# Queries of two mixers projected with channels on the partitions instead of tokens, in a two-layer decoder trunk

## The chip, the cores and the metric

The kernel runs on one core of a Trainium2 chip. The time is the device time of one execution in microseconds. A core has five engines that run side by side and wait for each other by semaphores: TensorE (PE, matmuls), VectorE (DVE), ScalarE (ACT), GpSimd (POOL) and SyncE (SP, which starts transfers). Each engine takes its own instructions strictly in the order in which the program lists them. PE reads two operands, a stationary one (at most 128 by 128) that it loads first, and a moving one of at most 512 columns, and writes into one of eight banks (PSUM), each 128 by 512 float32. Every other engine works on 128 partitions at a time.

## The reference

Two layers. Each layer is

```
h = rmsnorm(x); proj = h @ w_in                      # 512 tokens x 1024 -> 3072 columns
a_u, a_v, b_q, b_k, b_v, b_g, c_q, c_k, c_v = split(proj)
y_a = gmlp(a_u, a_v)                                 # 4 heads of 64
y_b = silu(b_g) * head_norm(retention(rope(b_q), rope(b_k), b_v))     # 6 heads of 64
y_c = sliding_window_attention_with_sinks(rope16(c_q), rope16(c_k), c_v)  # 6 query heads, 2 key heads
x += rmsnorm([y_a | y_b | y_c] @ w_out)
x += rmsnorm((silu(h2 @ w_gate_ffn) * (h2 @ w_up)) @ w_down)           # h2 = rmsnorm(x)
x += sigmoid(x @ w_gate) * rmsnorm(p @ w_ple)
```

The attention mixer (called swa below) works in chunks of 128 queries against the chunk's own and the previous 128 keys; softmax includes a sink. Retention (ret) works in chunks of 128 as well, with a running state. `rope` turns pairs of channels of a head by an angle that grows with the token: all 64 channels of a head in retention, the first 16 in attention. Everything is float32; the large matmuls are made of three products of a high and a low part (`mm3`), with operands of the type float32r.

## The kernel before, in words

Tokens are in four tiles of 128. The matrix `w_in` is taken in groups of columns (`GROUPS`): keys and values of attention (`ckv`, 256 columns), its queries (`cq`, 384), then keys, queries and values of retention (`bk`, `bq`, `bv`, 384 each), the gMLP (`a`, 512) and the retention gate (`bg`, 384). A group of 384 or 512 columns is two strips of four 128-row blocks. A strip is loaded by SP into `raw` (two pieces), split by ACT into `w_hi` (L1411) and by DVE into `w_lo` (L1891, L1893), and then PE runs four blocks on it, one for each tile of tokens (`mm_in`): the stationary operand is a tile of h, the moving one the weights, and the result has tokens on the partitions. A block of a 384-column strip is 4 x 3 = 12 matmuls. There are three slots of split weights, so the split of a strip starts when the strip three before it is used up.

The small work of the mixers is laid between these blocks. `plan_mixers` is a table by units: unit u is the u-th block of a layer's projection, counted from 4 (the first block after `ckv`), and behind the block of unit u every engine finds the steps that the table puts there, in the order of the `put` calls. The table says nothing of times; each engine simply takes its own part of each step in that order and waits by semaphore for what it needs. The steps of chunk c of attention are: `swa_T` (PE transposes queries and keys of a tile, L1255 and L1257, ACT copies them to `cT`), `swa_cur` (scores against the own keys, L1273; ACT copies them to `prob`, L1674), `swa_prev` (scores against the previous keys into the same banks, L1273; DVE merges and takes the maximum, L2258 to L2263; ACT takes the exponentials, L1682), `swa_norm` (DVE, L2268 to L2270), `swa_PT` (PE transposes the probabilities, L1281; ACT copies them to `ptu`, L1688 and L1691), `swa_mask` (DVE multiplies the transposed ones by a triangle, `ptl`, L2279), `swa_o` (PE, L1294), and `swa_yhi`, `swa_ylo` (ACT L1382 and DVE L1941 split the result). In `swa_PT` ACT copies one half, waits for DVE's mask of the other half (`pt_masked0`) and copies that; the copy of `swa_cur` of the next chunk is behind it in ACT's order, and PE's `swa_prev` of that next chunk waits for this copy (`swa_S`).

Retention has `ret_T` (transposes of key and query, L1309), `ret_sc` (scores L1317; DVE multiplies by a triangle into `scm`, L2289), `ret_o` (L1329, L1333, L1338; DVE adds to the state, L2303, and sums squares, L2306), `ret_norm` and `ret_yT`. Keys and queries of retention are rotated by DVE straight out of the banks (`rope_full`, L1920 to L1924, four instructions for a tile). Queries of attention come by ACT to `cq` (L1738) and are rotated by DVE there (L1934 to L1937). gMLP has `gmlp_v` (DVE, L2321 to L2328, five instructions for a tile; POOL L1838 and L1839 take the root of the variance) and `gmlp_n` (POOL, L1847 to L1849).

In the second layer the first blocks stand between the last ones of the layer before: transposes of x (L1214), splits to `h_hi` (ACT L1449) and `h_lo` (DVE L1957), and the split of the first weight strips.

## Time and profile before

| | us |
|---|---|
| median of 3 runs | 1225.45 (1225.24 to 1225.57) |
| the profiled execution | 1225.42 |
| its span, first to last instruction | 1223.7 |
| PE busy | 1217.0 |
| DVE busy | 841.5 |
| ACT busy | 616.0 |
| POOL busy | 136.6 |
| mean granted TensorE clock | 1.00 |

The span is what the trace covers; the 1.7 us between it and the time lie before the first and behind the last instruction. The projection and mixers of the first layer lie between 10 and 178 us, those of the second between 616 and 785 us. A timeline's row has start, duration, engine, line, operation, output and inputs, shape and count, and behind it in brackets the idle time before it with what ended it. Durations of matmuls are modelled to their end and overlap; the distance between two starts is what one costs PE.

### The profile page before, as it was taken

Reading aid. Unit: us, or ns where it says so; the run is one execution under the profiler, and the core shown is the slowest. Engines: PE = TensorE matmul, PEld = TensorE weight load, DVE = VectorE, ACT = ScalarE, POOL = GpSimd, SP = SyncE. Lnnn points to the kernel's source line nnn. Section 1 sums busy time; section 2 is a strip of 40 time slices with the busy share of each in tenths; the row PEclk is TensorE's granted clock in tenths of the full one; section 3 lists DMA queues with packets and bytes.
Section 4 is the critical chain, followed back from the end, with each engine's and each line's share of the span. In section 5 each row is a group of like instructions: output and inputs, shape, how many; then the busy total and the mean of one; then the engine's idle time right before and its main releaser. Section 6 shows DMA issues by size and latency. Waiting matters only on the chain.

```text
span 1223.7 us, 20397 instructions
## 1 busy us (share of the span) xinstructions
PE 1217.0 (99%) x7873; PEld 1109.8 (91%) x7873; DVE 841.5 (69%) x1365; ACT 616.0 (50%) x1204; POOL 136.6 (11%) x208
## 2 busy tenths in 40 slices
PE   9999999999999999999999999999999999999998
PEld 8988888999999988888899889889999999888887
DVE  5685646888888853267976756468988887433788
ACT  7454435555555532237664544364655555422474
POOL 2003621100000000003030037020000000000120
PEclk9999999999999999999999999999999999999999
DMA  7322232233333354320242222231333333444001
GB/s 247 111 65 91 70 103 69 70 104 104 104 105 106 109 183 154 124 67 18 86 119 73 91 75 90 74 103 53 104 105 106 108 101 119 163 147 172 18 18 70
DMA packets 124464, 122.31 MB, mean 100 GB/s; under 512 B 5200, under 2 KB 108752, under 8 KB 124368
## 3 DMA queue, kind: packets, MB, share of 16 engines
q1 hardware_dynamic: 123680, 120.48, 31.4%
q8 instruction: 63, 1.03, 0.4%
q10 hardware_dynamic: 688, 0.53, 0.2%
q14 instruction: 33, 0.27, 0.1%
HBM read 118.90 MB, written 2.10 MB: 99 GB/s over the span
## 4 chain that ended last, share of the span: by engine, by line
PE 98%; DVE 1%; ACT 0%; POOL 0%; issue 0%; DVEq 0%; ACTq 0%
PE bank L1004 31%; PE bank L1006 30%; PE bank L1005 30%; PE bank L1214 2%; PE bank L1273 1%; PE bank L1294 1%; PE bank L1333 1%; PE bank L1317 1%; PE bank L1309 0%; PE bank L1281 0%; PE bank L1329 0%; PE bank L1338 0%; PE bank L1224 0%; PE bank L1359 0%; PE bank L1255 0%; DVE ple_n L2196 0%
## 5 line engine op out<-in xcount | busy, mean ns | idle before, releaser
L1004 PE MATMUL bank<-w_hi,h_hi 128*128 128x384 f32 (+2 forms) x564 | 200.4, 355 | 0.8 <-DVE w_lo L1893 0.7
L1005 PE MATMUL bank<-w_lo,h_hi 128*128 128x384 f32 (+2 forms) x564 | 194.6, 345 | 0.0
L1891 DVE TENSOR_TENSOR w_lo<-raw,w_hi 128x1024 fp32r<-128x1024 f32 x70 | 83.6, 1233 | 133.7 <-ACT w_hi L1411 133.5
L1004 PE MATMUL bank<-h_hi,w_hi 128*128 128x256 f32 x568 | 161.0, 284 | 0.1
L1006 PE MATMUL bank<-h_hi,w_lo 128*128 128x256 f32 x568 | 160.7, 283 | 0.0
L1005 PE MATMUL bank<-h_lo,w_hi 128*128 128x256 f32 x568 | 160.7, 283 | 0.0
L1006 PE MATMUL bank<-w_hi,h_lo 128*128 128x384 f32 (+2 forms) x468 | 157.5, 336 | 0.0
L1411 ACT ACTIVATE w_hi<-raw 128x1024 fp32r<-128x1024 f32 x70 | 70.6, 1053 | 160.7 <-PE bank L1006 160.6
L1006 PE MATMUL bank<-w_hi,mid_lo 128*128 128x512 f32 x352 | 137.0, 389 | 0.0
L1004 PE MATMUL bank<-T_hi,w_hi 128*128 128x256 f32 x448 | 126.8, 283 | 0.0
L1005 PE MATMUL bank<-T_lo,w_hi 128*128 128x256 f32 x448 | 126.8, 283 | 0.0
L1006 PE MATMUL bank<-T_hi,w_lo 128*128 128x256 f32 x448 | 126.8, 283 | 0.0
L1004 PEld LDWEIGHTS bank<-w_hi,h_hi 128*128 128x128 f32 x564 | 106.2, 188 | 15.1 <-issue 5.2
L1005 PEld LDWEIGHTS bank<-w_lo,h_hi 128*128 128x128 f32 x564 | 106.3, 189 | 6.2
L1004 PEld LDWEIGHTS bank<-h_hi,w_hi 128*128 128x128 f32 x568 | 109.0, 192 | 0.6 <-issue 0.5
L1005 PEld LDWEIGHTS bank<-h_lo,w_hi 128*128 128x128 f32 x568 | 109.0, 192 | 0.1
L1006 PEld LDWEIGHTS bank<-h_hi,w_lo 128*128 128x128 f32 x568 | 109.0, 192 | 0.0
L1790 POOL TENSOR_SCALAR tiny<-tiny 128x1 f32<-128x1 f32 x24 | 20.0, 835 | 755.5 <-ACT junk_f L1614 683.0
L1505 ACT ACTIVATE w_hi<-w_sum 128x512 fp32r<-128x512 f32 x112 | 70.4, 629 | 52.5 <-DVE w_sum L2034 51.2
L1006 PEld LDWEIGHTS bank<-w_hi,h_lo 128*128 128x128 f32 x468 | 88.1, 188 | 3.1
L1004 PEld LDWEIGHTS bank<-T_hi,w_hi 128*128 128x128 f32 x448 | 86.0, 192 | 0.0
L1005 PEld LDWEIGHTS bank<-T_lo,w_hi 128*128 128x128 f32 x448 | 86.0, 192 | 0.0
(294 smaller groups left out, 2909.3 us busy)
## 6 DMA issues: line engine op xcount, KB each, us to landing
raw<-in_w_ffn_in SPq DMA_DIRECT2D x88, 512.0 KB, 3.9
raw<-in_w_ffn_out SPq DMA_DIRECT2D x44, 512.0 KB, 4.2
raw<-in_w_in SPq DMA_DIRECT2D x40, 384.0 KB, 3.8
raw<-in_w_out SPq DMA_DIRECT2D x16, 512.0 KB, 3.8
gw<-in_w_gate SPq DMA_DIRECT2D x16, 512.0 KB, 3.4
raw<-in_w_in SPq DMA_DIRECT2D x10, 512.0 KB, 4.6
raw<-in_w_ple SPq DMA_DIRECT2D x4, 512.0 KB, 5.9
x<-in_x_in SPq DMA_DIRECT2D x3, 512.0 KB, 6.9
```

Of the source, the lines that this page charges most:

```text
L1004: pe.matmul(out_ap, a_hi, b_hi, start=start, stop=False, skip_group_check=True)
L1005: pe.matmul(out_ap, a_hi, b_lo, start=False, stop=False, skip_group_check=True)
L1006: return pe.matmul(out_ap, a_lo, b_hi, start=False, stop=stop, skip_group_check=True)
L1214: last = pe.transpose(t_bank(layer, stage, m, half)[:, k * P:(k + 1) * P], src[:, kk * P:(kk + 1) * P], T_("ident"))
L1273: last = pe.matmul(swa_bank(c, g)[:, j * P:(j + 1) * P], cT[rows(g), j, ts(c)], cT[rows(g), 3, ts(k0)], start=True, stop=True, skip_group_ ...
L1294: last = pe.matmul(swa_bank(c, 1)[rows(g), 0:BW], values[:, g, :], probs[:, 3 * g:3 * g + 3, :], start=(i == 0), stop=(i == len(pairs) - 1 ...
L1317: last = pe.matmul(banks[4 + g][:, j * P:(j + 1) * P], kqT[rows(g), 0, j, :], kqT[rows(g), 1, j, :], start=True, stop=True, skip_group_che ...
L1333: last = pe.matmul(banks[4][:, cols], scm[:, g, j, :], bv[:, c, cols], start=(c == 0), stop=True, skip_group_check=True)
L1411: last = act.activation(w_hi[slot_of(g)][:, j * n + cols.start:j * n + cols.stop], raw[q % RAWS][:, cols], ACT.Copy, scale=1.0 if col is N ...
L1505: act.activation(hi, whole, ACT.Copy).then_inc(st_hi, 1)
L1790: pool.tensor_scalar(e_post[n % 2], ss_post[n % 2][:, 0:1], EPS, None, ALU.add).then_inc(post_e, 1)
L1891: last = dve.tensor_tensor(lo, raw[q % RAWS][:, cols], hi, ALU.subtract)
```

## The change

Queries of both mixers are now projected turned: the weights are the stationary operand (128 columns of them), h of all 512 tokens is the moving one, and the result has channels on the partitions. For this the queries' columns are put together (`turned_last`, on the host) and taken as three strips of 256 columns (`qa`, `qb`, `qc`), each two blocks of 128 channels; blocks 0 to 2 are attention, 3 to 5 retention. A unit is now half a block (4 x 3 = 12 matmuls of 512 columns). ACT copies a block to `q_raw`, POOL's queue starts four transfers that write it to `q_turn` with the halves of each rotated range exchanged, and DVE makes x cos + exchanged x sin from tables (`turns`) that SP loads. The copies, rotations and transposes of queries before are gone, and the tokens' norm factor enters at the exponentials (`s_q`, `s_qn`). In the second layer the first block is made for three tiles of tokens (`q_most`) ahead of the last block of `ckv`, and for the last tile behind it. A layer's projection has 48 units in place of 52; the table of steps is moved to match. The variances of `gmlp_v` go to two buffers in turn. The masks of chunks 0 and 1 are put one unit earlier.

```diff
-    "cq": (2 * AW + 4 * BW, BW),
+    "qa": (2 * AW + 3 * BW, 2 * P),
+    "qb": (2 * AW + 3 * BW + 2 * P, 2 * P),
+    "qc": (2 * AW + 3 * BW + 4 * P, 2 * P),
...
-    "bq": (2 * AW, BW),
...
+    for i in range(2 * len(TURNED)):
+        put((6, 8, 10, 12, 16, 17)[i], "q_rope", i)
+    put(8, "swa_T")
     for c in range(TILES):
-        put(10 + c, "swa_T", c)
         u = (13, 18, 23, 28)[c]
         put(u, "swa_cur", c)
...
         put(u + (2, 1, 2, 2)[c], "swa_norm", c)
+        put(u + (5, 4, 4, 5)[c], "swa_mask", c)
         put(u + 5, "swa_PT", c)
-        put(u + (5, 5, 3, 5)[c], "swa_mask", c)
         put(u + 7, "swa_o", c)
...
-        u = (33, 37, 41, 45)[c]
+        u = (31, 35, 39, 43)[c]
         for step, name in zip((0, 2, 3), ("ret_T", "ret_sc", "ret_o")):
             put(u + step, name, c)
-        put(41 + c, "gmlp_v", c)
-        put(42 + c, "gmlp_n", c)
+        put(37 + c, "gmlp_v", c)
+        put(38 + c, "gmlp_n", c)
...
+            add("q_most", lay=nxt)
+            mm(ins[0], 3, nxt)
             mm(ins[1], 0, nxt)
             mm(ins[1], 1, nxt)
-            mm(ins[0], 3, nxt)
...
+            def mm_turned(layer, i, half, cols):
+                g = layer * NS + SIDX[("in", TURNED[i // 2], 0)]
+                if half == 0 and i < 4:
+                    pe.wait_ge(*evac(layer, "ckv", i))
+                elif half == 0:
+                    pe.wait_ge(q_evac, 6 * layer + i - 3)
...
+                for k in range(4 * half, 4 * half + 4):
+                    last = mm3(banks[i % 4][:, cols], hi[:, k, c], lo[:, k, c], h_hi[:, k, cols], h_lo[:, k, cols],
+                               k == 0, k == KD - 1)
...
+                    if name == "bk":
+                        pe.wait_ge(q_evac, 6 * layer + (5, 6, 3, 4)[m])
...
+                        act.wait_ge(mm_done, mm_count(layer, strip, m))
+                        if n > 2:
+                            act.wait_ge(q_roped, n - 2)
+                        act.activation(q_raw[b][:], banks[i % 4][:, :], ACT.Copy).then_inc(q_evac, 1)
...
+                    pool.wait_ge(q_evac, 6 * layer + i + 1)
+                    for r in (0, HD):
+                        for d in (r, r + half):
+                            src = 2 * r + half - d
+                            pool.dma_start(q_turn[b][d:d + half, :],
+                                           q_raw[b][src:src + half, :]).then_inc(q_turned[b], 16)
...
+                    dve.tensor_tensor(dst, q_raw[b][:], cos_q[which][:], ALU.mult)
+                    dve.wait_ge(q_turned[b], 64 * (3 * layer + i // 2 + 1))
+                    step(dve.tensor_tensor(q_turn[b][:], q_turn[b][:], sin_q[which][:], ALU.mult))
+                    done(dve.tensor_tensor(dst, dst, q_turn[b][:], ALU.add), q_roped)
...
-                    for i, src in enumerate((bk, bq)):
-                        for j in range(3):
-                            last = pe.transpose(banks[4 + i][:, j * P:(j + 1) * P],
-                                                src[:, c, j * P:(j + 1) * P], T_("ident"))
+                    for j in range(3):
+                        last = pe.transpose(banks[4][:, j * P:(j + 1) * P], bk[:, c, j * P:(j + 1) * P], T_("ident"))
...
-                    if m or layer:
-                        dve.wait_ge(gm_r, layer * TILES + m)
-                    done(dve.tensor_reduce(gvar, heads(vsq[:], A_HEADS), AX.X, ALU.add), gm_v)
+                    if m > 1 or layer:
+                        dve.wait_ge(gm_r, layer * TILES + m - 1)
+                    done(dve.tensor_reduce(gvar[m % 2], heads(vsq[:], A_HEADS), AX.X, ALU.add), gm_v)
```

The first place at which instructions move, on DVE in each layer, is around the mask of chunk 1 (`ptl_103`). In DVE's order before, the last instruction of the norm (`prob_101`), one split of weights (`w_lo_79`) and then the mask:

```order
L2270 TENSOR_TENSOR prob_101<-prob_101,tiny 128x768 [waits dve_step]
L1893 SCALAR_TENSOR_TENSOR w_lo_79<-raw_74,mix_col,w_hi_76 128x384 [waits hi_ready]
L1893 SCALAR_TENSOR_TENSOR w_lo_79<-raw_74,mix_col,w_hi_76 128x384
L1893 SCALAR_TENSOR_TENSOR w_lo_79<-raw_70,mix_col,w_hi_76 128x384 [waits hi_ready]
L1893 SCALAR_TENSOR_TENSOR w_lo_79<-raw_70,mix_col,w_hi_76 128x384
L2279 TENSOR_TENSOR ptl_103<-bank,tab 128x384 [waits swa_PT]
L2279 TENSOR_TENSOR ptl_103<-bank,tab 128x384 [waits pt_copied1]
L1893 SCALAR_TENSOR_TENSOR w_lo_80<-raw_71,mix_col,w_hi_77 128x384 [waits hi_ready]
L1893 SCALAR_TENSOR_TENSOR w_lo_80<-raw_71,mix_col,w_hi_77 128x384
```

In DVE's order of the change the norm and the same split stand there too (line numbers are 69 to 81 higher), then four instructions for tile 0 of retention's keys as those of the first four rows here, and then, for tiles 1 and 2 (`rope_a`, `rope_b` and `bk`; L1988 and L1989 were L1920 and L1921), up to the mask and the start of tile 3:

```order
L1988 TENSOR_TENSOR rope_a<-bank,tab 128x384 [waits b_roped,mm_done]
L1989 TENSOR_TENSOR rope_b<-bank,tab 128x384
L1991 TENSOR_TENSOR bk<-rope_a,rope_b 128x6x32 [waits evac_dve]
L1992 TENSOR_TENSOR bk<-rope_a,rope_b 128x6x32
L1988 TENSOR_TENSOR rope_a<-bank,tab 128x384 [waits b_roped,mm_done]
L1989 TENSOR_TENSOR rope_b<-bank,tab 128x384
L1991 TENSOR_TENSOR bk<-rope_a,rope_b 128x6x32 [waits evac_dve]
L1992 TENSOR_TENSOR bk<-rope_a,rope_b 128x6x32
L2360 TENSOR_TENSOR ptl_103<-bank,tab 128x384 [waits swa_PT]
L2360 TENSOR_TENSOR ptl_103<-bank,tab 128x384 [waits pt_copied1]
L1988 TENSOR_TENSOR rope_a<-bank,tab 128x384 [waits b_roped,mm_done]
L1989 TENSOR_TENSOR rope_b<-bank,tab 128x384
```

The key rotations of tiles 0 to 2, which stood in the units of chunk 0 before, now stand between chunk 1's norm and chunk 1's mask; that of tile 3 is behind the mask.

The second place, on DVE as well, is the triangle product of retention's chunk 2 (`scm`). Before, it stands behind the gMLP step of tile 1 (`uv` to `vn` to `vsq`), ahead of that of tile 2:

```order
L2321 TENSOR_REDUCE tiny<-uv 128x4 [waits evac_act]
L2322 TENSOR_SCALAR tiny<-tiny 128x4 [waits dve_step]
L2323 TENSOR_TENSOR vn<-uv,tiny 128x256 [waits dve_step]
L2325 TENSOR_TENSOR vsq<-vn 128x256 [waits dve_step]
L2328 TENSOR_REDUCE tiny<-vsq 128x4 [waits gm_r,dve_step]
L2289 TENSOR_TENSOR scm<-bank,tab 128x384 [waits ret_sc]
L2289 TENSOR_TENSOR scm<-bank,tab 128x384
L2321 TENSOR_REDUCE tiny<-uv 128x4 [waits evac_act]
```

In the change it stands behind the steps of tiles 1, 2 and 3 and a split of weights of `w_out` (`w_lo_78`); the first row here is the end of tile 2's step:

```order
L2409 TENSOR_REDUCE tiny<-vsq 128x4 [waits gm_r,dve_step]
L1960 TENSOR_TENSOR w_lo_78<-raw_74,w_hi_75 128x1024 [waits hi_ready]
L1960 TENSOR_TENSOR w_lo_78<-raw_70,w_hi_75 128x1024 [waits hi_ready]
L2402 TENSOR_REDUCE tiny<-uv 128x4 [waits evac_act]
L2403 TENSOR_SCALAR tiny<-tiny 128x4 [waits dve_step]
L2404 TENSOR_TENSOR vn<-uv,tiny 128x256 [waits dve_step]
L2406 TENSOR_TENSOR vsq<-vn 128x256 [waits dve_step]
L2409 TENSOR_REDUCE tiny<-vsq 128x4 [waits gm_r,dve_step]
L2370 TENSOR_TENSOR scm<-bank,tab 128x384 [waits ret_sc]
L2370 TENSOR_TENSOR scm<-bank,tab 128x384
```

Two steps of gMLP and one split of weights have moved from behind the triangle product of chunk 2 to ahead of it.

## Rows read from the trace of the kernel before

**Rows 1.** Page: busy time of an engine, share of the span, instructions
```profile
PE 1217.0 (99%) x7873; PEld 1109.8 (91%) x7873; DVE 841.5 (69%) x1365; ACT 616.0 (50%) x1204; POOL 136.6 (11%) x208
```
**Rows 2.** Page: the chain that ended last, shares of the span by engine
```profile
PE 98%; DVE 1%; ACT 0%; POOL 0%; issue 0%; DVEq 0%; ACTq 0%
```
**Rows 3.** Timeline of PE: 384-column matmuls, then 512-column ones of w_out
```profile
22.88 0.34 PE L1004 MATMUL bank<-w_hi,h_hi 128*128 128x384 f32 x1
...
37.27 0.34 PE L1006 MATMUL bank<-w_hi,h_lo 128*128 128x384 f32 x1
...
180.56 0.39 PE L1004 MATMUL bank<-w_hi,y_hi 128*128 128x512 f32 x1
...
185.78 0.39 PE L1006 MATMUL bank<-w_hi,y_lo 128*128 128x512 f32 x1
```
**Rows 4.** Chain in order of time, first layer: start, duration, engine, line
```profile
37.61 0.33 PE bank L1255 x3
40.14 0.33 PE bank L1255 x3
...
111.83 1.28 PE bank L1333 x12
...
116.62 0.66 PE bank L1309 x6
```
**Rows 5.** Timeline of DVE at the start of layer two
```profile
603.68 3.25 DVE L1893 SCALAR_TENSOR_TENSOR w_lo<-raw,mix_col,w_hi 128x256 fp32r<-128x256 f32 x8
...
619.98 2.20 DVE L1893 SCALAR_TENSOR_TENSOR w_lo<-raw,mix_col,w_hi 128x384 fp32r<-128x384 f32 x4
...
622.61 1.28 DVE L1957 TENSOR_TENSOR h_lo<-bank,h_hi 128x512 fp32r<-128x512 f32 x2
```
**Rows 6.** Timeline of PE there, behind the last transposes
```profile
623.35 0.39 PE L1004 MATMUL bank<-w_hi,h_hi 128*128 128x256 f32 x1
```
**Rows 7.** Chain in order of time: swa_o of chunk 0, swa_prev of chunk 2
```profile
64.08 0.80 PE bank L1294 x4
...
75.16 0.87 PE bank L1273 x12
```
**Rows 8.** Timeline of DVE: key rotations to mask 0, norm 1 to split
```profile
55.59 0.55 DVE L1920 TENSOR_TENSOR rope_a<-bank,tab 128x384 f32<-128x384 f32 x1
...
60.75 1.01 DVE L2279 TENSOR_TENSOR ptl<-bank,tab 128x384 f32<-128x384 f32 x2
...
63.27 1.05 DVE L2258 COPY_PREDICATED prob<-later_m,bank 128x384 f32<-128x384 int32 x2
...
68.28 0.17 DVE L2268 TENSOR_TENSOR tiny<-tiny 128x6 f32<-128x6 f32 x1 [2.12 <-ACT tiny L1684]
...
69.59 2.20 DVE L1893 SCALAR_TENSOR_TENSOR w_lo<-raw,mix_col,w_hi 128x384 fp32r<-128x384 f32 x4
```
**Rows 9.** Timeline of ACT: copies of ptu and prob, chunk 2 to 3
```profile
87.50 0.49 ACT L1691 ACTIVATE ptu<-bank 128x384 f32<-128x384 f32 x1
87.89 0.87 ACT L1674 ACTIVATE prob<-bank 128x384 f32<-128x384 f32 x2
```
**Rows 10.** Timeline of DVE: retention's chunk 1, gMLP tiles 0 and 2
```profile
129.28 0.72 DVE L2303 TENSOR_TENSOR state<-state,bank 64x192 f32<-64x192 f32 x2 [2.48 <-PE bank L1338]
...
130.50 0.41 DVE L2321 TENSOR_REDUCE tiny<-uv 128x4 f32<-128x256 f32 x1
...
132.12 0.42 DVE L2328 TENSOR_REDUCE tiny<-vsq 128x4 f32<-128x256 f32 x1
...
139.97 0.41 DVE L2321 TENSOR_REDUCE tiny<-uv 128x4 f32<-128x256 f32 x1
...
142.70 2.35 DVE L1891 TENSOR_TENSOR w_lo<-raw,w_hi 128x1024 fp32r<-128x1024 f32 x2
```
**Rows 11.** Transfers issued: KB each, median us from issue to landing
```profile
raw<-in_w_in SPq DMA_DIRECT2D x40, 384.0 KB, 3.8
...
later_m<-in_later SPq DMA_DIRECT2D x1, 64.0 KB, 9.3
```
**Rows 12.** Timeline of SP's queue: one issue near the start
```profile
4.38 0.43 SPq L976 DMA_DIRECT2D tab<-in_table  x1
```

More of the change, by code:

```diff
@@ L200, in plan_schedule @@
         mm(o[0], 0)
-        for u in (52, 53):
-            if u == 53:
+        for u in (48, 49):
+            if u == 49:
                 mm(o[1], 0)
@@ L519, in build_trunk @@
     r_mix = [small(1) for _ in range(TILES)]
+    s_q = [small(1) for _ in range(TILES)]
+    s_qn = [small(1) for _ in range(TILES)]
     nsnk = small(C_HEADS)
@@ L533, in build_trunk @@
     gmu = small(4)
-    gvar = small(4)
+    gvar = [small(4) for _ in range(2)]
     gvt = small(4)
@@ L579, in build_trunk @@
     ck_roped = sem("ck_roped")
-    cq_roped = sem("cq_roped")
+    turns_loaded = [sem(f"turns_loaded{i}") for i in range(2)]
+    q_evac = sem("q_evac")
+    q_turned = [sem(f"q_turned{i}") for i in range(2)]
+    q_roped = sem("q_roped")
+    q_scaled = sem("q_scaled")
+    q_zeroed = sem("q_zeroed")
     b_roped = sem("b_roped")
@@ L1161, in block_of @@
                     pe.wait_ge(lo_ready, 2 * (g + 1))
-                if kind == "in":
+                if kind == "in" and strip[1] in TURNED:
+                    block = 2 * TURNED.index(strip[1]) + m // 2
+                    last = mm_turned(layer, block, m % 2, slice(S - P if layer and block == 0 else 0, S))
+                elif kind == "in":
                     last = mm_in(layer, g, strip, m)
@@ L1246, in _ @@
                     gate_product(layer, e[1], e[2:] or (0, 1))
+                elif kind == "q_most":
+                    for half in range(2):
+                        mm_turned(layer, 0, half, slice(0, S - P))
                 elif kind == "swa_T":
-                    c = e[1]
-                    pe.wait_ge(ck_roped, layer * TILES + c + 1)
-                    pe.wait_ge(cq_roped, layer * TILES + c + 1)
-                    if c > 1:
-                        pe.wait_ge(swa_cT, layer * TILES + c - 1)
-                    for j in range(3):
-                        pe.transpose(banks[6 + c % 2][:, j * P:(j + 1) * P], cq[c % 2][:, j * P:(j + 1) * P],
-                                     T_("ident"))
-                    pe.transpose(banks[6 + c % 2][:, 3 * P:4 * P], ck[:, c, :],
-                                 T_("ident")).then_inc(swa_T, 1)
+                    pe.wait_ge(ck_roped, (layer + 1) * TILES)
+                    for c in range(TILES):
+                        last = pe.transpose(banks[6][:, c * P:(c + 1) * P], ck[:, c, :], T_("ident"))
+                    last.then_inc(swa_T, 1)
                 elif kind in ("swa_cur", "swa_prev"):
@@ L1313, in _ @@
                     c = e[1]
-                    pe.wait_ge(ret_kqT, layer * TILES + c + 1)
+                    pe.wait_ge(ret_kT, layer * TILES + c + 1)
+                    if c == 0:
+                        pe.wait_ge(q_roped, 6 * layer + 6)
                     for j in range(3):
                         for g in range(2):
-                            last = pe.matmul(banks[4 + g][:, j * P:(j + 1) * P], kqT[rows(g), 0, j, :],
-                                             kqT[rows(g), 1, j, :], start=True, stop=True,
+                            last = pe.matmul(banks[4 + g][:, j * P:(j + 1) * P], kT[rows(g), j, :],
+                                             qT[rows(g), j, ts(c)], start=True, stop=True,
                                              skip_group_check=True)
@@ L1699, in _ @@
                     act.wait_ge(ret_T, layer * TILES + c + 1)
-                    for i in range(2):
-                        last = act.activation(kqT[:, i, :, :],
-                                              banks[4 + i][:, 0:BW].rearrange("p (k t) -> p k t", k=3),
-                                              ACT.Copy)
-                    last.then_inc(ret_kqT, 1)
+                    act.activation(kT[:], banks[4][:, 0:BW].rearrange("p (k t) -> p k t", k=3),
+                                   ACT.Copy).then_inc(ret_kT, 1)
                 elif kind == "ret_o":
@@ L1909, in pre, with rope_full @@
                                                   op0=ALU.mult, op1=ALU.mult), xn_ready)
-            def rope_full(layer, which, m):
-                dst = (bk, bq)[which]
+            def rope_full(m):
                 xr = banks[m][:, 0:BW].rearrange("p (h s d) -> p h s d", h=6, s=2)
@@ L2363, in _, with turned_last @@
                         dve.wait_ge(mm_done, mm_count(layer, strip, m))
-                        rope_full(layer, DVE_EVAC.index(name), m)
+                        rope_full(m)
+def turned_last(w):
+    a, bq, bk, bv, bg, cq, ckv = np.split(w, np.cumsum([2 * AW] + 5 * [BW]), 2)
+    cq = cq.reshape(*w.shape[:2], C_KV, C_HEADS // C_KV, HD).transpose(0, 1, 3, 2, 4).reshape(cq.shape)
+    return np.concatenate([a, bk, bv, bg, cq, bq, ckv], 2)
 def heads_in_pairs(w):
@@ L2385 @@
     depth = w_in.shape[0]
-    table, later = small_tables()
+    table, later, turns = small_tables()
     values = {
```

136 lines of the change are left out of this document (90 added, 46 removed).

## The prediction

> **What bounds the kernel.** I read the busy shares first: PE works 1217.0 of the 1223.7 us of the span, DVE 841.5 [rows 1]. Then the chain that ended last: 98% of it is PE and DVE holds 1% [rows 2]. So the time is PE's work plus the few places where it waits, and each term below is either work taken from PE or a wait given to it. The profiled execution took 1225.42 us, 1.7 more than its span and 0.03 less than the median of the runs, so the sum is made against 1225.42. The granted clock is 1.00 throughout, which is the 2.4 GHz level; the work ahead of the changed stages stays as dense, so I leave it there.
>
> **PE's work, projection.** Two matmuls of 384 columns 83 apart start at 22.88 and 37.27: 0.1734 us each. Two of 512 columns 23 apart start at 180.56 and 185.78: 0.2270 each [rows 3]. The queries were 2 groups x 8 blocks x 12 = 192 matmuls of 384 columns, 33.29 us; they become 6 x 2 x 12 = 144 of 512, 32.68 us. Layer 1: -0.6. In layer 2 the first block is cut in two: 24 matmuls for three tiles (384 columns, 4.16 us) and 24 for the last tile (128 columns), beside 120 of 512 (27.24 us). The trace has no float32r matmul of 128 columns. By the slope of columns between 384 and 512 one would cost 0.067; if it were as dear as one of 384 it would cost 0.173. The nearest row is the smaller matmul of retention, 12 in 1.28 us, 0.107 each although it has 64 columns [rows 4]; I take that: 2.57 us (ends 1.6 and 4.2). Layer 2 is 33.97 us, +0.7.
>
> The row of 64 columns shows that a matmul doesn't fall with its columns below some cost. The Trainium skill, "TensorE: Matmul & The Clock Gate", section on LDWEIGHTS, gives P/1.2 ns for loading P columns of stationary operand, 107 ns for 128, and with it this row agrees; its section on the back-to-back issue gap says about 81 ns for N=128, by which the last tile would cost 1.9 us in place of 2.57 and the sum would be 0.6 lower.
>
> **PE's work, transposes.** Each layer had four groups (`swa_T`) of four transposes; one group stays, for the keys. From one group to the next 2.53 us pass [rows 4], of which 12 x 0.1734 = 2.08 are a block: 0.45 a group, so -1.35 a layer. Retention's six transposes for a chunk take 0.66 us [rows 4]; three stay, -0.33 for each of four chunks, -1.32 a layer. PE's work together: layer 1 -3.28, layer 2 -1.99, in all -5.3 us.
>
> **Start of layer 2.** DVE splits the first strip of queries there. A split of a 384-column piece is four instructions in 2.20 us, of 256-column strips eight in 3.25 [rows 5]; the strip of the change is of the second kind, so DVE comes 1.05 later to `h_lo` of tile 2. That instruction starts at 622.61 and its first half is done at 623.25; PE wants it at 623.35 [rows 5, 6]. Spare is 0.1, so PE stands 0.9 to 1.05: +1.0, once.
>
> **Mask of chunk 1, both layers.** Three key rotations now stand ahead of it on DVE. I count from the end of `swa_o` of chunk 0, 64.08 + 0.80 = 64.88, since the order on PE between it and `swa_prev` of chunk 2 keeps its length; PE starts that one at 75.16, 10.28 later [rows 7]. DVE's chain from 64.88: to the norm's start at 68.28, 3.4 (0.3 less if ACT's exponentials come straight behind its copy of y, since rotations no longer hold DVE's maximum); norm to the split 1.31; split 2.1 to 2.2; three rotations, 60.75 - 55.59 = 5.16; half of a mask 0.5 [rows 8]. Then ACT's second copy to `ptu` (0.39 to the next start) and its copy of the scores, 0.87 [rows 9]; this last is what PE waits for. Sum 13.4 to 13.8 against 10.28: PE stands 3.1 to 3.5 us, and as some of it may be off the path I take 3.2; +6.4 for two layers. Queued behind the mask on DVE are the last key rotation and the maximum for chunk 2; both have time while PE stands. The end from below is 0 for each, if DVE runs further ahead of PE than I count.
>
> **`scm` of retention's chunk 2, both layers.** Two gMLP steps and a split for `w_out` are now ahead of it. From the end of `ret_o` 1, DVE: state and sum 1.22; three gMLP steps at 2.0 each (130.50 to 132.12 + 0.42) or, as at 139.97 to 142.70, 2.73; a split of 2.35; `scm` 1.0, the same operation and size as a mask [rows 8, 10]. That is 10.5 to 12. PE meanwhile: a block of 512 columns 2.72, three transposes 0.33, two blocks of 2.08, scores 0.87, a block 2.08: 10.2. Stall 0 to 1.8, I take 1.2: +2.4 for two layers. The second variance buffer takes from DVE's last instruction of a gMLP step the wait for POOL's root, for which reason I count the steps without such waits; beyond that it is worth nothing by itself, since nothing of PE's hangs on gMLP there.
>
> **Transfers of POOL's queue.** The trace has no transfer from POOL's queue. From above and below: in SP's queue an issue takes 0.43 [rows 12], landings take 3.8 at the median for 384 KB and 9.3 at the start for 64 KB, which is the size here [rows 11]. Four issues and the common landing are 5.5 us; with the long one 11. What waits is DVE's rotation of block 3; behind it in DVE's order stand the merge and maximum of chunk 0, behind these ACT's exponentials, and behind them in ACT's order the copy of the last query block, whose bank PE needs for the second block of keys. PE takes from the end of block 3 to there four half blocks (10.9), a block of keys (2.08) and two scores (0.87 each) [rows 3, 7]: 14.7. The others need a copy (0.49 for 384 columns [rows 9], 0.65 for 512), two DVE instructions of 512 columns (0.55 each for 384, 1.5 together), merge to exponentials 68.28 - 63.27 = 5.0 [rows 8], and a copy, 0.65: 7.8, with some 0.6 as an estimate for the hand-overs 8.4. That leaves 6.3 us for the transfers before PE stands. I take 5.5: hidden, 0. If they take longer, each microsecond costs PE one in each layer. The first layer's extra strips, ACT's copies of queries (it is busy 50% of the span) and the loads of tables (four of 256 KB a layer) lie beside PE's work: 0.
>
> The Trainium skill, "DMA: Bandwidth & Descriptors", section on the anatomy of a GpSimd-path DMA, gives about 2.0 us + bytes/436e3 each, thus by estimate 8.6 us for four of 64 KB one behind another, 2.3 past the slack; no row here shows it. "SBUF — State Buffer" adds that some DVE modes starve the writing of descriptors, which no run shows either.
>
> **Sum.** -5.3 + 1.0 + 6.4 + 2.4 + 0 = +4.5; 1225.42 + 4.5 = 1229.9 us. About 0.2%, 2.45 us, is what a measurement of this kernel tells from no change.
>
> **Rivals.**
> A. The masks and `scm` are in time: the new waits don't come, or only the 1.0 and a rest. For it: DVE is busy 69% of the span, and before the norm of chunk 1 it idled 2.12 us waiting for ACT [rows 8], a wait that may shrink by more than my 0.3. The point is the mask of chunk 1: from a chain of 10.28 us down the 6.4 are gone, and they are the price. Against: the wait of 2.12 ends with ACT, whose work stays, and 5.16 us of rotations are more than it. Time 1225.4 - 5.3 + 0 to 2.4 = 1220.1 to 1222.5. Chance 0.20. This is the case in which the change gains.
> B. Half of the stalls, which is what the lower ends of my counts leave, if PE's way is longer by hand-overs of its own: 1225.4 - 5.3 + 1 + 3.2 + 1.2 = 1225.5, 1223 to 1227.9: no difference. Chance 0.16.
> C. Late transfers: the place is the bank of the last query block, the point is a landing over 6.3 us after the copy, the price (d - 6.3) x 2. At d = 8.6 as with slow landings, +4.6: 1234.5; at 11, +9: 1239. Against: SP's landings of 3.8. Chance 0.14, slower still than mine.
> D. The forecast: 1227.9 to 1233, chance 0.50.
>
> Slower by over 0.2%: C and D, 0.64; within: 0.16; faster: 0.20. The range reaches from inside A to C, 1221.5 to 1235; the likeliest case's own is 1227.9 to 1233.
>
> **What the changed profile would show.** PE busy falls by some 5 us to about 1212, its idle time rises from 6.7 to about 16. In the chain, PE's `swa_prev` of chunk 2 follows ACT's copy to `prob`, behind DVE's mask, in both layers, with 3 us of wait each; without these waits the term of 6.4 is wrong. The score product of retention's chunk 2 is followed by DVE's gMLP steps and split, and `ret_o` 2 waits about 1 us. At the start of layer 2 `h_lo` of tile 2 holds the third `ckv` block for 1 us. The 24 matmuls of 128 columns start 0.107 apart. Each fourth transfer of a query block has landed under 6.3 us after ACT's copy, and PE never waits for `q_evac` at the keys; a longer landing there means case C. A span that falls while all DVE steps come late would prove the order on PE to have more slack than 10.28.

## The result and the profile after

The changed kernel takes 1235.65 us (median of four runs, 1234.17 to 1236.11), the one before 1225.45: ratio 1.0081, 95% interval 1.0064 to 1.0099. It is slower, as forecast, but by 10.2 us in place of 4.5, and outside the range of 1221.5 to 1235.0. The page of the profile after, busy time and share of the span of each engine:

```profile
span 1233.6 us, 20244 instructions
PE 1217.7 (99%) x7753; PEld 1098.2 (89%) x7753; DVE 849.5 (69%) x1353; ACT 617.4 (50%) x1210; POOL 168.9 (14%) x276
```

The share of PE is 99% as in [rows 1], and says nothing of what happened. The chain that ended last does: PE had 98% of it [rows 2].

```profile
PE 93%; DVE 4%; ACT 1%; issue 1%; POOL 0%; DVEq 0%; ACTq 0%
```

The view of waits, for PE: who waited, for whom, the sum in us, how often, the longest. These five of its rows matter; the second and the fifth were there before with 1.2 and 0.7, and the rows left out differ from before by 0.3 us or less.

```profile
PE bank L1324 <- ACT prob L1722: 7.3, 2, 3.6
PE bank L1277 <- DVE still L2014: 1.2, 1, 1.2
PE bank L1380 <- DVE scm L2370: 1.1, 2, 0.6
PE bank L1036 <- DVE h_lo L2025: 0.8, 1, 0.8
PE bank L1036 <- DVE ple_n L2264: 0.7, 2, 0.4
```

All three waits that the prediction named are there, and no other new one: 7.3 + 1.1 + 0.8 = 9.2 us. PE's idle time, span less busy, went from 6.7 to 15.9 us, which is the same 9.2. The rest of the result is PE's busy time: it should have fallen by 5.3 and rose by 0.7. The windows of the same trace show why (start and end of a stretch, its length, busy time of PE, PEld, DVE, ACT, POOL, then the granted clock):

```profile
85.00:91.00 6.00, 5.50 (x24) 5.06 (x24) 5.45 (x11) 2.88 (x6) 0.00 (x0) 0.50 0.24 67
92.00:97.00 5.00, 5.00 (x30) 4.35 (x27) 1.09 (x4) 3.45 (x14) 0.00 (x0) 1.00 0.14 50
699.00:703.00 4.00, 4.00 (x20) 3.71 (x18) 3.52 (x7) 1.89 (x4) 0.00 (x0) 0.57 0.16 26
```

Behind each of the two waits at the scores of chunk 2 (they end at 85.50 and 698.50) the clock stands at 0.50, the 1.2 GHz level: for 6.8 us in layer 1 (84.7 to 91.5), the first 0.8 of them still idle, and for 3.4 us in layer 2 (699.1 to 702.5). The rows of PE there:

```profile
85.50 1.65 PE L1324 MATMUL bank<-cT 64*128 64x128 f32 x12 [3.63 <-ACT prob L1722]
87.08 0.69 PE L1036 MATMUL bank<-w_hi,h_hi 128*128 128x384 f32 x1
87.56 0.52 PE L1037 MATMUL bank<-w_lo,h_hi 128*128 128x384 f32 x1
87.88 0.52 PE L1038 MATMUL bank<-w_hi,h_lo 128*128 128x384 f32 x1
```

The twelve score matmuls take 1.65 us, 0.87 before [rows 7], and 384-column matmuls start 0.32 apart and not 0.1734 [rows 3]. PE works for 6.0 and 3.4 us of these at half speed, which costs 3.0 and 1.7, together 4.7 us. Idle time and slow clock are 13.9 us, and the span grew by 9.9 (1233.6 - 1223.7). So 4.0 us of work were saved net; this last number is what is left over and not a measurement of its own. `best6` below measures the saving without new waits. Another 0.4 us is outside the span (2.2 between span and time, 1.7 before).

The wait at the mask, followed on DVE:

```profile
75.03 0.17 DVE L2349 TENSOR_TENSOR tiny<-tiny 128x6 f32<-128x6 f32 x1 [2.40 <-ACT tiny L1733]
...
76.33 2.20 DVE L1962 SCALAR_TENSOR_TENSOR w_lo<-raw,mix_col,w_hi 128x384 fp32r<-128x384 f32 x4
78.44 0.55 DVE L1988 TENSOR_TENSOR rope_a<-bank,tab 128x384 f32<-128x384 f32 x1
...
80.22 0.56 DVE L1988 TENSOR_TENSOR rope_a<-bank,tab 128x384 f32<-128x384 f32 x1
...
82.01 0.56 DVE L1988 TENSOR_TENSOR rope_a<-bank,tab 128x384 f32<-128x384 f32 x1
...
83.61 1.01 DVE L2360 TENSOR_TENSOR ptl<-bank,tab 128x384 f32<-128x384 f32 x2
```

Against [rows 8]: norm, split, three rotations 1.78 us apart (from the first to the mask 83.61 - 78.44 = 5.17, forecast 5.16), mask. ACT waits for it and copies:

```profile
84.19 0.49 ACT L1740 ACTIVATE ptu<-bank 128x384 f32<-128x384 f32 x1 [5.05 <-DVE ptl L2360]
84.58 0.87 ACT L1722 ACTIVATE prob<-bank 128x384 f32<-128x384 f32 x2
```

From the end of `swa_o` 0 (71.5) to the end of this copy (85.45) are 13.95 us; PE wanted it after 10.4 (85.50 - 3.63 - 71.5).

The rows that answer to the remaining terms: `scm` of retention's chunk 2, and PE behind it; `h_lo` of tile 2 in layer 2; the first of 24 matmuls of 128 columns and the 512-column one behind the last.

```profile
144.08 2.54 DVE L1960 TENSOR_TENSOR w_lo<-raw,w_hi 128x1024 fp32r<-128x1024 f32 x2
...
148.95 1.02 DVE L2370 TENSOR_TENSOR scm<-bank,tab 128x384 f32<-128x384 f32 x2
```
```profile
150.03 0.49 PE L1380 MATMUL bank<-state,qT 128*128 128x128 f32 x2 [0.56 <-DVE scm L2370]
...
628.76 0.39 PE L1036 MATMUL bank<-w_hi,h_hi 128*128 128x256 f32 x1 [0.83 <-DVE h_lo L2025]
...
638.77 0.22 PE L1036 MATMUL bank<-h_hi,w_hi 128*128 128x128 f32 x1
...
641.40 0.44 PE L1036 MATMUL bank<-h_hi,w_hi 128*128 128x512 f32 x1
```

The 24 take 2.63 us, 0.110 each (0.107 was taken from a 64-column row of [rows 4]). And the transfers of POOL's queue, which no row of before showed: four issues a block, and from the page's list of transfers size and landing.

```profile
40.95 2.05 POOL L1870 DMA_DIRECT2D q_turn<-q_raw  x4 [3.88 <-ACT q_raw L1781]
```
```profile
q_turn<-q_raw POOLq DMA_DIRECT2D x24, 64.0 KB, 2.0
q_turn<-q_raw POOLq DMA_DIRECT2D x24, 16.0 KB, 2.0
```

An issue takes 0.5 us, a landing 2.0 at the median and 3.5 at most; DVE's product waits until 44.26, 3.6 us after the copy's end at 40.66. DVE waits three times for such a landing, 6.2 us together, PE never.

### The profile page after: what moved, and what is told of

It is laid out like the page before. It is cut to its first block, busy times and chain, and to the rows that moved or that the text cites. A ratio compares the mean times of both kernels' runs of the same rounds, so it can differ in the third digit from the quotient of the medians.

```text
span 1233.6 us, 20244 instructions
## 1 busy us (share of the span) xinstructions
PE 1217.7 (99%) x7753; PEld 1098.2 (89%) x7753; DVE 849.5 (69%) x1353; ACT 617.4 (50%) x1210; POOL 168.9 (14%) x276
## 4 chain that ended last, share of the span: by engine, by line
PE 93%; DVE 4%; ACT 1%; issue 1%; POOL 0%; DVEq 0%; ACTq 0%
PE bank L1036 29%; PE bank L1038 29%; PE bank L1037 29%; PE bank L1267 2%; PE bank L1324 1%; PE bank L1345 1%; PE bank L1384 1%; DVE w_lo L1962 1%; ACT prob L1731 0%; PE bank L1368 0%; PE bank L1380 0%; DVE w_lo L1960 0%; PE bank L1389 0%; PE bank L1332 0%; PE bank L1277 0%
## 5 line engine op out<-in xcount | busy, mean ns | idle before, releaser
L1036 PE MATMUL bank<-h_hi,w_hi 128*128 128x256 f32 (+2 forms) x672 | 200.6, 299 | 0.1
L1038 PE MATMUL bank<-h_hi,w_lo 128*128 128x256 f32 (+2 forms) x672 | 200.0, 298 | 0.0
L1037 PE MATMUL bank<-h_lo,w_hi 128*128 128x256 f32 (+2 forms) x672 | 199.9, 297 | 0.0
L1036 PE MATMUL bank<-w_hi,h_hi 128*128 128x384 f32 (+2 forms) x436 | 158.4, 363 | 1.4 <-DVE h_lo L2025 0.8
L1037 PE MATMUL bank<-w_lo,h_hi 128*128 128x384 f32 (+2 forms) x436 | 153.1, 351 | 0.0
L1036 PEld LDWEIGHTS bank<-h_hi,w_hi 128*128 128x128 f32 x672 | 128.6, 191 | 4.1 <-issue 0.5
L1038 PE MATMUL bank<-w_hi,h_lo 128*128 128x384 f32 (+2 forms) x340 | 115.9, 341 | 0.0
L1036 PEld LDWEIGHTS bank<-w_hi,h_hi 128*128 128x128 f32 x436 | 83.1, 191 | 16.3 <-issue 6.1
L1037 PEld LDWEIGHTS bank<-w_lo,h_hi 128*128 128x128 f32 x436 | 83.2, 191 | 6.3
L1038 PEld LDWEIGHTS bank<-T_hi,w_lo 128*128 128x128 f32 x448 | 86.0, 192 | 0.0
```

What stands on the lines that cost most here:

```text
L1036: pe.matmul(out_ap, a_hi, b_hi, start=start, stop=False, skip_group_check=True)
L1037: pe.matmul(out_ap, a_hi, b_lo, start=False, stop=False, skip_group_check=True)
L1038: return pe.matmul(out_ap, a_lo, b_hi, start=False, stop=stop, skip_group_check=True)
```

## The experiments

Two theories stood at the start. By the first, called A in most expectations, the loss is DVE's order (one mask behind three rotations), and the slow clock follows from the idle. By the second, other parts of the change (turned blocks, transfers, a second buffer) have a share. Sixteen kernels were run. Where nothing else is said an experiment is an edit of the changed kernel's table of steps.

**Where the mask stands.** Three kernels move the mask of chunk 1 alone (`mold` has also the mask of chunk 2 one unit earlier).

```diff
-        put(u + (5, 4, 4, 5)[c], "swa_mask", c)
+        put(u + (5, 5, 3, 5)[c], "swa_mask", c)     # mold: behind 4 rotations
+        put(u + (5, 3, 4, 5)[c], "swa_mask", c)     # m21:  behind 2
+        put(u + (5, 2, 4, 5)[c], "swa_mask", c)     # m20:  behind 1
```

> The change with its masks at the old units (one later for chunks 1, one earlier for 2): the mask of chunk 1 is now behind all four key rotations. Theory A (each rotation ahead of the mask costs PE its 1.78 us): the wait at the scores of chunk 2 grows from 3.6 to 5.4 us in each layer, 3.6 us more in all, 1239 us; the mask of chunk 2 ahead of its transposes' neighbours costs nothing. Rival B: the last key rotation was in the wait's shadow anyway; same as the change, 1235.5.

> Mask of chunk 1 one unit earlier on DVE: behind the key rotations of tiles 0 and 1 (1.78 us less ahead of it than in the change). Theory A: PE waits 3.6 - 1.8 = 1.8 us at the scores of chunk 2 in each layer, so 3.6 us less than the change; if an idle of 1.8 us is too little to bring the clock down, another 5 are saved: 1227; if it isn't, half the slow stretch stays: 1229.5. Rival B (the clock has nothing to do with the wait): 1232.0 with the same two slow stretches of 6.4 and 3.3 us.

> Mask of chunk 1 two units earlier on DVE: behind the key rotation of tile 0 instead of those of tiles 0 to 2 (2 x 1.78 us less ahead of it). Theory A (the loss is the mask: 7.3 us of waiting at the previous-key scores of chunk 2, and the stretch at the 1.2 GHz level behind it comes from that idle): the wait falls below 0.5 us per layer, the granted clock stays 1.00, time 1235.65 - 7.3 - 5 = about 1223.5 us. Rival B (the clock falls for another reason, such as the denser 512-column stretch ahead of it): the waits go but the clock still falls, about 1228.4. Rival C (the rotations that now stand behind the mask hold the banks that the value blocks need): waits of 1 to 2 us at the blocks of bv in each layer, 1225.5 to 1227.5.

Measured: `mold` 1239.68 us (ratio 1.0116, 1.0101 to 1.0131), `m21` 1230.78 (1.0045, 1.0030 to 1.0060), `m20` 1233.15 (1.0064, 1.0048 to 1.0079). The wait at the scores of chunk 2 was 5.43 us a layer behind four rotations, 3.63 behind three, 1.85 behind two: 1.78 to 1.80 for each rotation, as theory A has it. With one it is gone, but `m20` is slower than `m21` and far from the 1223.5 expected, which neither of its rivals foresaw. Its largest wait of PE, and DVE's split and norm of chunk 2 with PE behind them:

```profile
PE bank L1332 <- DVE prob L2351: 5.7, 2, 2.8
```
```profile
85.83 2.74 DVE L1962 SCALAR_TENSOR_TENSOR w_lo<-raw,mix_col,w_hi 128x512 fp32r<-128x512 f32 x4
...
94.56 0.96 DVE L2351 TENSOR_TENSOR prob<-prob,tiny 128x768 f32<-128x768 f32 x1
...
95.58 0.88 PE L1332 MATMUL bank<-tab,prob 128*128 128x128 f32 x6 [2.83 <-DVE prob L2351]
```

PE now stands at the transposes of chunk 2 (L1332) until DVE has done that chunk's norm. In DVE's order between the two norms are two splits (2.2 and 2.7 us), four rotations, a mask and the maximum, and behind the maximum DVE waits for ACT's exponentials (3.1 us). That is more than PE's work takes from the one norm to the other; in the change the wait at the scores had hidden this. The mask was the first of two late links of one overfull stretch.

**The two smaller waits.** `m20gm` puts the gMLP steps two units later, and `best1` has, on top, the low part of h of tile 2 ahead of the split of the first strip of queries in layer 2.

```diff
-        put(37 + c, "gmlp_v", c)
-        put(38 + c, "gmlp_n", c)
+        put(39 + c, "gmlp_v", c)
+        put(40 + c, "gmlp_n", c)
...
-            add("conv", SIDX[ins[1]], lay=nxt)
             mm(ins[0], 0, nxt)
             add("T", "mix", 2, lay=nxt)
             add("pre", "mix", 2, lay=nxt)
+            add("conv", SIDX[ins[1]], lay=nxt)
```

> As the one with the mask behind one rotation, and the gMLP steps two units later, so that the triangle product of retention's chunk 2 stands ahead of the steps of tiles 2 and 3 and of the split for w_out. Theory A: the two waits of 0.6 and 0.5 us go, 1.1 less than that kernel, 1222.4. Rival: the gMLP's last steps come later and hold the gMLP product or the norms of retention in the w_out stretch; no gain or up to 2 us lost, 1223.5 to 1225.5.

> As the one before, and in layer 2 the low part of h of tile 2 stands ahead of the split of the first strip of queries on ACT and DVE. Theory A: the third ckv block of layer 2 no longer waits, 1.0 us less, 1221.4. Rival: the split of 3.25 us is now too late for the first query block (it starts 3 us after the third ckv block), and the wait only moves there: 1222.4 or up to 1 us more.

`m20gm` measured 1232.65 us (1.0063, 1.0048 to 1.0078): the wait for `scm` went from 1.1 to 0.8 only, as one gMLP step and the split now stand just ahead of it, and the time can't be told from `m20`'s. `best1`: 1230.78 (1.0044, 1.0027 to 1.0061). The wait for `h_lo`, 0.9 us, is gone and came back nowhere; the other 1 us between the two lies within their intervals.

**The splits on that stretch.** `best2` is `best1` with both splits of weights behind the maximum of chunk 2. On top of it `best2g` has a single variance buffer, and `best2sp` has each transfer cut in four.

```diff
+                if u == 24:
+                    close(ins[4])
+                    close(ins[5])
                 u += 1
-            close(s)
+            if s not in ins[4:6]:
+                close(s)
```

> As the kernel with early mask, later gMLP steps and the earlier low part in layer 2, and the two splits of weights that follow the key blocks are moved behind the maximum of chunk 2, where DVE otherwise idles about 2.7 us for ACT's exponentials. Theory A (DVE's chain from the norm of chunk 1 to the norm of chunk 2 is too long by 2.8 us for PE, and 2.2 + 2.7 us of it are splits that can lie in that idle): the wait of PE for the norm of chunk 2 goes in both layers (5.7 us in that kernel), and with it the stretches at the 1.2 GHz level; 1230.8 - 5.7 - 3 = about 1222. Rival B (the work is only shifted and chunk 3 is late instead): a wait of 1 to 3 us for chunk 3's norm or mask in each layer, 1224 to 1229. Rival C (a split becomes late for the value blocks): PE waits for w_lo at bv.

> The same kernel as the first of this group with one variance buffer in place of two (DVE waits again for POOL's root before it writes the sum of squares of the next tile). Theory A (hidden by itself, as the prediction has it): within 0.5 us. Rival: DVE is now on the path in that stretch, and the wait of about 1.2 us a step delays the triangle product of retention: 1 to 3 us more.

> The same kernel with each of the four transfers of a query block cut by columns into four: 16 issues of POOL's queue at 0.5 us each in place of four, so the last lands about 10 us after the copy instead of 3.6. The prediction's count gave 6.3 us until PE stands. Theory A: (10 - 6.3) x 2 = 7.4 us more, and some 3 to 5 more if the clock falls behind each such idle: 8 to 12 us over the uncut kernel. Rival (slack is longer, or issues of a quarter are cheaper): under 3 us more.

`best2`: 1236.98 us (1.0092, 1.0077 to 1.0107), worse by 6 than what it was made from, where about 1222 was expected. Rival C (a split too late for the value blocks) had half of it:

```profile
PE bank L1336 <- DVE prob L2355: 4.9, 2, 3.2
PE bank L1040 <- DVE w_lo L1966: 4.3, 3, 1.9
```
```profile
91.26 4.98 DVE L1966 SCALAR_TENSOR_TENSOR w_lo<-raw,mix_col,w_hi 128x384 fp32r<-128x384 f32 x8 [4.15 <-ACT w_hi L1466]
```

A split has a high part on ACT and a low part on DVE. Moved together, ACT's part fell behind its exponentials, DVE idled 4.15 us for it, and the value blocks and the norm were both late.

`best2g`: 1236.70 us against 1236.98 (intervals 1.0072 to 1.0106 and 1.0077 to 1.0107): the second variance buffer alone is worth nothing here, as forecast. `best2sp`: 1266.39 (1.0329, 1.0314 to 1.0345), 29 us over `best2` where 8 to 12 were expected. The expectation looked at one block's delay. But 16 issues at 0.5 us are 8 us of POOL's queue for each block, and PE makes a block in 5.45, so the backlog grows over the six blocks, and the queue issued without a pause for 35 us:

```profile
29.39 35.08 POOL L1875 DMA_DIRECT2D q_turn<-q_raw  x69 [2.17 <-ACT q_raw L1785]
```

PE waited 11.4 and 8.9 us in sum at two new places, and its busy time rose by 9.5 us over `best2`'s, with seven stretches at the 1.2 GHz level in place of three.

**High part early, low part late.** `best3` keeps ACT's part of the two splits in place and moves DVE's, the first behind the maximum of chunk 2 and the second three units later. It also puts the gMLP steps of tiles 1 to 3 at units 42 to 44, behind retention's third triangle product. `best3m22` is `best3` with the mask of chunk 1 alone put back behind three rotations, and `best3sp2` is `best3` with each transfer cut in two.

```diff
+                if u in (24, 27):
+                    add("lo", SIDX[ins[u // 3 - 4]] + SLOTS)
                 u += 1
-            close(s)
+            if s in ins[4:6]:
+                add("hi", SIDX[s] + SLOTS)
+            else:
+                close(s)
...
-        put(37 + c, "gmlp_v", c)
-        put(38 + c, "gmlp_n", c)
+        put((39, 42, 43, 44)[c], "gmlp_v", c)
+        put((40, 43, 44, 45)[c], "gmlp_n", c)
```

> Mask of chunk 1 behind one rotation; of the splits behind the key blocks only DVE's low part is late (behind the maximum of chunk 2, and behind its mask), ACT's high part stays early, so that DVE needn't wait for it; gMLP steps of tiles 1 to 3 behind retention's third triangle product; low part of h of tile 2 first in layer 2. Theory A: DVE reaches the norm of chunk 2 at about 92 us, when PE wants it at 92.7; the waits of 5.7 (the early mask's) and 0.8 us and both slow stretches go, what stays is PE's saving of 5.3: 1220 to 1222 us. Rival: a remainder of 0.5 to 1 us a layer at the norm of chunk 2 or at chunk 3: 1222 to 1224.

> The same kernel with the mask of chunk 1 back behind three rotations, alone. Theory A: a rotation ahead costs 1.78 us, the split of 2.2 that has gone from there gives as much back, so PE waits 3.6 - 2.1 = 1.5 us at the scores of chunk 2 in each layer: 3.0 more than the kernel it is made from, and up to 3.3 more if even such an idle is followed by a stretch at 1.2 GHz. Rival (the mask's place is unimportant once the splits are gone): under 1 us more.

> The same kernel with each transfer of a query block cut into two: 8 issues of 0.5 us each, the last landing about 4.1 + 2.0 = 6 us after the copy instead of 3.6, and the queue's 4.1 us a block is still under PE's 5.45. Theory A (the prediction's count of 6.3 us until PE stands): at the edge, 0 to 1 us more. Rival (DVE already waits for transfers in three places, so each microsecond reaches PE): 2.4 us and more for each layer, 5 us or more.

`best3`: 1227.93 us (1.0026, 1.0015 to 1.0036), where 1220 to 1222 was expected. The waits at chunk 2 are gone. The largest that are left in the mixers:

```profile
PE bank L1385 <- DVE scm L2375: 3.6, 2, 1.8
PE bank L1364 <- DVE y_lo L2014: 1.0, 2, 0.6
```

The later gMLP steps now hold the last triangle product. `best3m22`: 1231.24 (1.0048, 1.0035 to 1.0061), 3.3 over `best3`; PE stands 1.62 us twice at the scores, 1.5 expected: the mask's place costs the same in another order. `best3sp2`: 1235.20 (1.0081, 1.0068 to 1.0094), 7.3 over `best3`, so the rival had it. In layer 1 the landing that counts came 8.8 us after its copy and not 6, since the last of the eight issues landed only 4.3 us after it was made. PE stood 3.7 us, so the slack there is 8.8 - 3.7 = 5.1 us, not 6.3. In layer 2 it is 7.1 - 1.2 = 5.9. With the 3.6 of the change at least 1.5 us are in hand.

**Is it the idle that brings the clock down?** In two kernels nothing is turned: the kernel before gets ten or five extra products on DVE ahead of that mask.

```diff
+                    if c == 1:
+                        landed(spent.get("rope"))
+                        for _ in range(10):
+                            step(dve.tensor_tensor(rope_a[:], rope_b[:], rope_b[:], ALU.mult))
                     dve.wait_ge(swa_PT, layer * TILES + c + 1)
```

> The kernel before, with ten extra products of 384 columns into a scratch tile on DVE ahead of the mask of chunk 1 in each layer (about 0.5 us each). DVE had 1.3 us to spare there, so PE stands about 3.7 us at the scores of chunk 2. Theory A (the idle itself brings the clock down): behind it a stretch at 1.2 GHz of 3 to 7 us in each layer, costing 1.6 to 3.3 each; 1225.4 + 7.4 + 3.2 to 6.6 = 1236 to 1239.5. Rival (only turned blocks ahead of an idle do this): clock 1.00, 1232.8.

> The same with five products: an idle of about 1.2 us in each layer. Theory A: an idle of about 1.8 us brought the clock down in the other kernels and 0.5 did not, so this tells where between: 1227.8 with the clock at 1.00, 1231 to 1234 with the slow stretches. Rival as before: 1227.8.

`oldlate10`: 1239.05 us (1.0114, 1.0099 to 1.0130), PE idle 4.4 us twice (an extra product took 0.59, not 0.5). `oldlate5`: 1228.94 (1.0029, 1.0018 to 1.0041), idle 1.4 us twice. Windows of the first, then of the second, behind the wait of layer 1:

```profile
80.00:84.00 4.00, 4.00 (x21) 3.78 (x20) 3.32 (x7) 1.62 (x4) 0.00 (x0) 0.50 0.23 48
85.00:90.00 5.00, 5.00 (x29) 3.82 (x28) 3.99 (x11) 2.90 (x14) 0.47 (x1) 1.00 0.18 67
```
```profile
78.00:82.00 4.00, 4.00 (x23) 2.79 (x22) 3.97 (x10) 1.24 (x3) 0.38 (x1) 1.00 0.47 132
```

With 1.4 us the clock stays at 1.00 and the kernel loses little more than it waits (3.6 for 2.8). With 4.4 us the clock falls in both layers, for 6.8 and 3.4 us, and the kernel loses 13.7 for 8.8. Of the 4.9 between, PE's busy time in the trace accounts for 4.2 (1221.2 against 1217.0); that trace is of the fastest of four executions. The extra products are in both kernels and nothing is turned in either, so the length of the idle is what differs.

**Does the saving exist?** Three orders more, each made to take away the waits that the last one left. `best4` has the gMLP step of tile 3 at unit 46 and one more low part late. `best5` has that step at unit 45 and the low part of the strip after the last value block late too. `best6` has the gMLP steps spread earlier. The edit shown is from `best3` to `best6`.

```diff
-                if u in (24, 27):
+                if u in (24, 27, 30, 34):
-                    add("lo", SIDX[ins[u // 3 - 4]] + SLOTS)
+                    add("lo", SIDX[ins[{24: 4, 27: 5, 30: 6, 34: 7}[u]]] + SLOTS)
-            if s in ins[4:6]:
+            if s in ins[4:8]:
...
-        put((39, 42, 43, 44)[c], "gmlp_v", c)
-        put((40, 43, 44, 45)[c], "gmlp_n", c)
+        put((37, 38, 41, 43)[c], "gmlp_v", c)       # best5: 39, 42, 43, 45; best4: 39, 42, 43, 46
+        put((38, 39, 42, 44)[c], "gmlp_n", c)       # best5: 40, 43, 44, 46; best4: 40, 43, 44, 47
```

> As best3, with the gMLP step of tile 3 behind retention's last triangle product (it waited 1.8 us for DVE in each layer), and the low part of one more strip moved behind the norm of chunk 3 (PE waited 0.4 and 0.55 us for the low part of y of chunk 2). Theory A: with no wait left in the mixers PE's saving of 5.3 us shows: 1227.0 - 3.6 - 1.0 = 1222.4 where the clock holds at 1.00, 1220.5 to 1223. Rival: the moved steps open another wait of 1 us or more: 1223.5 to 1226.

> As best4, with the gMLP step of tile 3 one unit earlier (right behind retention's last triangle product, where DVE idled 2.9 us) and the low part of the strip after the last value block behind retention's chunk 0, where DVE idled 3.8 us. Theory A (the waits are all of DVE's order, and PE's saving is there): no wait over 0.5 us in the mixers, 1220.5 to 1223 where the clock holds at 1.00. Rival B (the saving is smaller than 5.3, as PE's changes of operand cost something too): no waits, but 1223 to 1225. Rival C: a new wait again, over 1225.

> As best5, with the gMLP steps spread earlier (tile 0 ahead of the triangle product of retention's chunk 1, where DVE idled 2.8 us, tile 1 behind its state, tiles 2 and 3 behind the product of chunk 2 and its state), so that POOL's last step is done before PE wants the gMLP product; it waited 1.76 us for it in each layer. Theory A: these 3.5 us go and nothing else comes: 1221.7 us, 0.9971 of the kernel before. Rival: the earlier steps delay the triangle product of chunk 1 or 2 again: 1222.5 to 1225.

`best4`: 1231.23 us (1.0048, 1.0035 to 1.0060), worse than `best3`: PE waits 3.4 us for the `scm` of retention's chunk 0 and 3.1 for a `y_lo`, as the moved pieces now stood ahead of those. `best5`: 1225.19 (0.9999, 0.9990 to 1.0008), one wait left in the mixers, 3.5 us for POOL's last gMLP step. `best6`: 1221.14 us (0.9965, 0.9951 to 0.9979), 4.3 us faster than the kernel before, where 1221.7 was expected. Busy times from its page, and its waits of PE:

```profile
PE 1212.3 (99%) x7753; PEld 1094.2 (90%) x7753; DVE 852.5 (70%) x1353; ACT 618.1 (51%) x1210; POOL 170.9 (14%) x276
```
```profile
PE bank L1282 <- DVE still L2019: 1.2, 1, 1.2
PE bank L1041 <- DVE ple_n L2269: 0.7, 2, 0.4
PE bank L1041 <- DVE w_lo L1967: 0.7, 2, 0.5
PE bank L1272 <- DMA x<-in_x_in: 0.2, 1, 0.2
```

No wait in the mixers is left, the clock stays at 1.00 there, and PE's busy time is 4.7 us under that of [rows 1]. The span is 4.7 us shorter too (1219.0). From the first matmul of `w_in` to the first of the feed-forward part PE takes 201.25 us in layer 1, in place of 204.27 (8.09 to 209.34, before 7.95 to 212.22). For layer 2, from the start of the gate ahead of it (`x @ w_gate`), it is 241.6 in place of 243.2. That is 3.0 and 1.7 us saved. The turned projection is thus a gain of about 0.35% (0.2 to 0.5 by the interval), and the change lost it in the order of DVE's work.

## Why the prediction missed

The direction, the three waits and their places were right; the size of the whole was not.

- **Clock, the step that failed.** The prediction read 1.00 in the profile of before and said of the granted clock, "so I leave it there". It gave PE 9.8 us of new idle and didn't ask what the clock does behind one. The clock fell to the 1.2 GHz level behind both long waits, and that cost 4.7 of the 5.7 us that were missing. It shows in the forecast of the profile as well: PE's idle time came out as forecast (15.9 us, about 16), and its busy time did not (1217.7, about 1212). `oldlate10` beside `oldlate5` shows that the long idle is the cause. No row of before could give the price, as PE never waited for longer than 1.2 us; but a cost with no row should have widened the range upwards.
- **Mask.** PE stood 3.63 us a layer; 3.1 to 3.5 were counted and 3.2 taken, 0.9 us too little in all. Of the 0.3 us that ACT's exponentials were to start earlier nothing came, and the deduction for parts "off the path" had no reason.
- **`scm`.** PE stood 0.56 us a layer, and 1.2 were taken (0 to 1.8). The three gMLP steps on DVE took 1.9, 1.9 and 2.4 us, where 2.0 to 2.73 each had been counted. The upper end was also added up wrongly: three steps of 2.73 give 12.8 us and a stall of 2.6, not 12 and 1.8.
- **`h_lo`.** PE stood 0.83 us against 1.0 forecast.
- **PE's saving.** 5.3 us were forecast. `best6` shows 4.7, 3.0 in layer 1 and 1.7 in layer 2 where 3.28 and 1.99 were forecast; the 128-column matmuls came as priced (0.110 us, 0.107 forecast), and where the missing 0.3 a layer is stays open. In the change only 4.0 are left over. Its waits may account for that: in `oldlate5` two waits with the clock at 1.00 raised PE's busy time by 1.0 us. No run shows it for the change itself.
- **Transfers.** The common landing came 3.6 us after the copy, 5.5 had been taken, and it is hidden as said. The slack was 5.1 and 5.9 us and not 6.3 (`best3sp2`). In the Trainium skill, "DMA: Bandwidth & Descriptors", section on the anatomy of a GpSimd-path DMA, the constant of about 2.0 us agrees with the median landing here. The prediction's estimate of 8.6 us had four transfers one behind another. They are not: each is issued 0.5 us after the last, and they are under way together. Rival C is refuted for the change as it is.
- **Rival A** (the mask in time) is refuted: 13.95 us against 10.4. **Rival B** (half of the stalls) is too, as the stalls came to 9.2 of 9.8 us. The prediction's last sentence, on more slack in PE's order, did not come true.
- The time outside the span grew by 0.4 us, which the sum had left at 1.7. Every kernel with the turned projection has this but `best2g`, the one with a single variance buffer, at 1.7. Why, stays open.

Account: 4.5 forecast + 4.7 clock + 0.9 mask - 1.3 `scm` - 0.2 `h_lo` + 1.3 saving + 0.4 outside the span = 10.3; measured 10.2.

What none of the steps saw is that the mask was only the first late link. Most repairs, taken alone, moved the wait: from the mask to the norm, from the norm to the value blocks, then to `scm`, `y_lo` and the gMLP.

## What to carry to other kernels

When a change makes the bounding engine wait, price the wait and then what TensorE's clock does behind it; in these traces a wait of 3.6 us cost 5.3 to 6.6. Before judging a change by its time, list the bounding engine's waits and repair the order of the others until none is new: here a change that measured 0.8% slower holds a gain of 0.35%. Where an operation is split between two engines, move only the half that stands in the way, and count a queue's issues against the time of a block, not only one transfer's delay.
